# A fourth weight block in the opening: values of the third unit of heads as a plain 32-bit product, with x transposed early and modulated in SBUF

## What is computed

```python
cond = silu(c)
for layer in range(2):
    mod = cond @ ada_w[layer] + ada_b[layer]              # 2048 x 12288 each
    sh1, sc1, g1, sh2, sc2, g2 = split(mod, 6)
    h = rms_norm(x) * (1.0 + sc1) + sh1
    y = even_mixer(h, ...) if layer == 0 else odd_mixer(h, ...)
    x = x + g1 * y
    h = rms_norm(x) * (1.0 + sc2) + sh2
    x = x + g2 * swiglu(h, ffn_w_in[layer], ffn_w_out[layer])
...
def even_mixer(h, w_in, w_out, ...):
    proj = h @ w_in                                        # 2048 x 6144
    aq, ak, av, bq, bk, bv = split(proj, ...)              # 12 blocks of 512 columns
    ...                                                    # heads, in four units of q, k, v
    return concatenate([ya, yb]) @ w_out
```

## Time and profile before

| | |
|---|---|
| median of 3 runs | 2210.9 us (2210.18 to 2211.12) |
| profiled execution: time, span | 2210.82 us, 2209.0 us |
| TensorE busy | 2136.7 us, 97% |
| VectorE busy | 1620.0 us, 73% |
| ScalarE busy | 986.1 us, 45% |
| memory read | 589.62 MB, mean 268 GB/s |

### The profile page before, as it was taken

How to read it: one execution, slowest core, us unless ns; L and a number is a source line. 1 busy time by engine, 2 the same in 40 slices (tenths; PEclk the granted TensorE clock), 3 DMA queues, 4 the chain that set the end, 5 groups by cost and what they waited for, 6 DMA issues and landing times.

```text
span 2209.0 us, 25961 instructions
## 1 busy us (share of the span) xinstructions
PE 2136.7 (97%) x9844; PEld 1755.8 (79%) x9844; DVE 1620.0 (73%) x1681; ACT 986.1 (45%) x1312; POOL 9.4 (0%) x21
## 2 busy tenths in 40 slices
PE   4799999999999999999999999999999999999998
PEld 3578888878888888888887877778888888888886
DVE  6999898988789988777667676686665555455546
ACT  4354444454443344434445456554444344434444
POOL 0000000000000000000000000000000000000000
PEclk7899999999999999999999999999999999999999
DMA  9978879859889999977755533458765555555543
GB/s 395 420 315 313 308 308 375 345 233 363 336 325 369 383 381 379 382 285 289 285 209 233 204 139 125 146 210 323 283 246 191 191 191 190 190 190 190 191 152 152
DMA packets 82557, 593.02 MB, mean 268 GB/s; under 512 B 9424, under 2 KB 9584, under 8 KB 10912
## 3 DMA queue, kind: packets, MB, share of 16 engines
q1 hardware_dynamic: 81216, 587.31, 69.4%
q0 software_dynamic: 1248, 4.44, 0.6%
HBM read 589.62 MB, written 2.10 MB: 268 GB/s over the span
## 4 chain that ended last, share of the span: by engine, by line
PE 83%; DVE 10%; DMA 3%; ACT 3%; DVEq 1%; issue 1%; SPq 0%; ACTq 0%
PE ps L1423 26%; PE ps L1425 26%; PE ps L1424 26%; DVE w_lo L837 3%; DMA ada_raw<-in_ada 2%; PE ps L1411 2%; DVE ada_raw L841 2%; DMA raw<-in_ab_in 1%; PE ps L1451 1%; PE ps L1453 1%; PE ps L1452 1%; ACT w_hi L490 1%; DVE work L981 1%; DVEq L980 0%; ACT ada_raw L594 0%
## 5 line engine op out<-in xcount | busy, mean ns | idle before, releaser
L837 DVE TENSOR_TENSOR w_lo<-raw,w_hi 128x1024 fp32r<-128x1024 f32 x728 | 878.9, 1223 | 409.5 <-ACT w_hi L490 405.2
L490 ACT ACTIVATE w_hi<-raw 128x1024 fp32r<-128x1024 f32 x728 | 762.3, 1059 | 933.8 <-PE ps L1425 753.7
L1423 PE MATMUL ps<-w_hi,xT_hi 128*128 128x512 f32 x1940 | 768.7, 396 | 27.6 <-DVE xT_lo L1141 25.8
L1425 PE MATMUL ps<-w_hi,xT_lo 128*128 128x512 f32 x1940 | 760.0, 392 | 0.0
L1424 PE MATMUL ps<-w_lo,xT_hi 128*128 128x512 f32 x1940 | 759.3, 391 | 0.0
L1423 PEld LDWEIGHTS ps<-w_hi,xT_hi 128*128 128x128 f32 x1940 | 366.7, 189 | 108.3 <-DVE xT_lo L1141 28.0
L1425 PEld LDWEIGHTS ps<-w_hi,xT_lo 128*128 128x128 f32 x1940 | 366.8, 189 | 78.0
L1424 PEld LDWEIGHTS ps<-w_lo,xT_hi 128*128 128x128 f32 x1940 | 367.4, 189 | 74.1
L841 DVE SCALAR_TENSOR_TENSOR ada_raw<-ada_raw,cond 128x2048 f32<-128x2048 f32 x176 | 402.0, 2285 | 8.9 <-DMA ada_raw<-in_ada 7.2
L1423 PE MATMUL ps<-w_hi,hT_hi 128*128 128x512 f32 x896 | 351.5, 392 | 0.1
L1425 PE MATMUL ps<-w_hi,hT_lo 128*128 128x512 f32 x896 | 348.8, 389 | 0.0
(11 more groups left out here) (185 smaller groups left out, 878.2 us busy)
## 6 DMA issues: line engine op xcount, KB each, us to landing
ada_raw<-in_ada SPq DMA_DIRECT2D x176, 1024.0 KB, 6.8
raw<-in_ffn_in SPq DMA_DIRECT2D x176, 1024.0 KB, 5.0
raw<-in_ffn_out SPq DMA_DIRECT2D x88, 1024.0 KB, 5.2
raw<-in_ab_in SPq DMA_DIRECT2D x48, 1024.0 KB, 8.9
raw<-in_swa_in SPq DMA_DIRECT2D x20, 1024.0 KB, 5.1
raw<-in_ab_out SPq DMA_DIRECT2D x16, 1024.0 KB, 7.4
raw<-in_swa_out SPq DMA_DIRECT2D x16, 1024.0 KB, 5.4
spare<-in_ada SPq DMA_DIRECT2D x8, 1024.0 KB, 9.0
```

The lines of the kernel that those rows point to most:

```text
L490: nc.scalar.activation(w_hi[:, p % PAIRS, :, :], raw[:, t % RAW, 2 * (p % 2):2 * (p % 2) + 2, :], ACT.Copy).then_inc(hi_ready, 1)
L837: tt(w_lo[:, p % PAIRS, :, :], raw[:, (p // 2) % RAW, 2 * (p % 2):2 * (p % 2) + 2, :], w_hi[:, p % PAIRS, :, :].bitcast(F32), ALU.subtract ...
L1423: mm(out, hi[:, kt, tok], w_hi[:, q % PAIRS, k, :], start=(kt == 2 * ps0), stop=False)
L1425: last = mm(out, lo[:, kt, tok], w_hi[:, q % PAIRS, k, :], start=False, stop=(kt == 2 * ps1 - 1))
```

## The change

Four things are changed.

*A fourth block.* Unit 2's values are not multiplied in the split form behind unit 1 any more. The opening does this block: four extra quads (`ab_early`) come through slot 3 of `raw` (`EARLY_RAW`), the other weights of unit 0 use a ring of three. TensorE multiplies them straight from `raw` with the modulated x in 32 bits (`early_pair`: four matmuls a round, into banks 6 and 7), without `hi` and `lo`. SP issues the first of these quads in round 0, the others at the end of rounds 2, 4 and 6, each after a wait for `early_used`, which TensorE raises with each group of four products. After the last group ScalarE copies the values to `v_early`, part of `xm`.

*x in SBUF.* `xm` (16 slices of 256 columns; it lies over `hT_lo`, which is used later) takes the transposed x. TensorE transposes the slices of rounds 2 to 7 right behind the three pairs of round 0, through banks 6 and 7, and ScalarE copies each to `xm` (`copy_x0`), between the normalisations. From round 1 on, ScalarE modulates in `xm`, and `xT_hi` and `xT_lo` are made out of it.

*Units 2 and 3 apart.* `AB23` becomes `AB2` (two blocks, 16 pairs) and `AB3` (three blocks). The modulation tiles of the three units are now 12, 8 and 14. The end of unit 1's attention (y to `hT`) and unit 2's key rotation move into unit 3; unit 2's attention lies five pairs later.

*Waits.* Unit 1's fourth quad waits for all eight products (slot 3), unit 0's key transposes wait for `early_copied`.

```diff
@@ sync
             def weights(ph, i, t):
                 sp.wait_ge(lo_ready, LO_CREDIT + 2 * (ph.quad(i, t) - ph.raw_distance(t) + 1))
-                sp.dma_start(raw[:, t % RAW, :, :].rearrange("p a n -> p (a n)"),
-                             T[ph.src][ph.src0 + i * ph.quads + t]).then_inc(raw_landed[t % RAW], 16)
+                if ph is AB1 and t == EARLY_RAW:
+                    sp.wait_ge(early_used, 8)
+                sp.dma_start(raw[:, t % ph.ring, :, :].rearrange("p a n -> p (a n)"),
+                             T[ph.src][ph.src0 + i * ph.quads + t]).then_inc(raw_landed[t % ph.ring], 16)
+
+            def early_weights(s):
+                if s:
+                    sp.wait_ge(early_used, 2 * s)
+                sp.dma_start(raw[:, EARLY_RAW, :, :].rearrange("p a n -> p (a n)"),
+                             T["ab_early"][s]).then_inc(raw_landed[EARLY_RAW], 16)
...
                 for t in range((3 * j + 1) // 2, (3 * j + 4) // 2):
                     weights(AB0, 0, t)
+                if j % 2 == 0:
+                    early_weights(j // 2)
@@ scalar
+            def copy_x0(j):
+
+                act.wait_ge(x0T_done, j + 1)
+                nc.scalar.activation(xm[:, 2 * j:2 * j + 2, :], bank(6 + j % 2).rearrange("p (k s) -> p k s", k=2),
+                                     ACT.Copy).then_inc(x0_copied, 1)
+
             for j in range(8):
                 if j == 7:
                     hi(AB0, 0, 21)
                 act.wait_ge(mods_ready, j + 1)
-                act.wait_ge(x0T_done, j + 1)
-                for k in range(2):
-                    kt = 2 * j + k
-                    o = ps[:, (6 + j % 2) * 512 + k * SEQ:(6 + j % 2) * 512 + (k + 1) * SEQ]
-                    last = nc.scalar.activation(o, o, ACT.Identity, bias=mod[:, 0, 0, kt:kt + 1],
+                if j:
+                    act.wait_ge(x0_copied, j)
+                else:
+                    act.wait_ge(x0T_done, 1)
+                for kt in range(2 * j, 2 * j + 2):
+                    src = xm[:, kt, :] if j else ps[:, 6 * 512 + kt * SEQ:6 * 512 + (kt + 1) * SEQ]
+                    last = nc.scalar.activation(xm[:, kt, :], src, ACT.Identity, bias=mod[:, 0, 0, kt:kt + 1],
                                                 scale=mod[:, 0, 1, kt:kt + 1])
...
                 if j == 0:
-                    normalise(2)
-                    normalise(3)
+                    copy_x0(1)
+                    for c in range(1, 4):
+                        normalise(c)
+                        copy_x0(2 * c)
+                        copy_x0(2 * c + 1)
             hi(AB1, 0, 0)
             copy_v(0)
+            act.wait_ge(early_used, 8)
+            nc.scalar.activation(v_early, bank(6, 2).rearrange("p (t n) -> p t n", t=TT), ACT.Copy).then_inc(early_copied, 1)
@@ tensor
+            def early_pair(j):
+
+                pe.wait_ge(raw_landed[EARLY_RAW], 16 * (j // 2 + 1))
+                for k in range(2):
+                    kt = 2 * j + k
+                    for t in range(TT):
+                        last = mm(bank(6 + t), xm[:, kt, t * P:(t + 1) * P], raw[:, EARLY_RAW, 2 * (j % 2) + k, :],
+                                  start=kt == 0, stop=kt == KT - 1)
+                last.then_inc(early_used, 1)
...
                 pe.wait_ge(x0l_done, j + 1)
                 for b in range(3):
                     pair(AB0, 0, b, j, AB0_SLOT[b], xT_hi, xT_lo, q=3 * j + b)
-                if j < 6:
-                    first_blocks(j + 2)
+                if j == 0:
+                    for c in range(2, 8):
+                        first_blocks(c)
+                    pe.wait_ge(x0_copied, 7)
+                early_pair(j)
@@ phases
-    AB1 = phase(1, 3, 8, 5, src="ab_in", src0=12, evacs=2, lag=4)
-    AB23 = phase(2, 3, 8, 6, src="ab_in", src0=24, evacs=2)
+    AB1 = phase(1, 3, 8, 6, src="ab_in", src0=12, evacs=2, lag=4)
+    AB2 = phase(1, 2, 8, 4, src="ab_in", src0=24, evacs=2)
+    AB3 = phase(1, 3, 8, 7, src="ab_in", src0=32, evacs=2)
```

More of the change, by code:

```diff
@@ L64, with __init__ @@
 class Phase:
-    def __init__(self, prev, n, blocks, pairs, ada, src=None, src0=0, evacs=None, lag=0, tiles_at=None):
+    def __init__(self, prev, n, blocks, pairs, ada, src=None, src0=0, evacs=None, lag=0, tiles_at=None,
+                 ring=RAW, fills=None):
         self.n, self.blocks, self.pairs, self.ada, self.lag, self.tiles_at = n, blocks, pairs, ada, lag, tiles_at
@@ L75, in __init__ @@
         self.ada0 = prev.ada0 + prev.n * prev.ada if prev else 0
-        self.fills = [len(range(s, self.quads, RAW)) for s in range(RAW)]
+        self.ring, self.after = ring, prev.ring if prev else RAW
+        self.fills = fills or [len(range(s, self.quads, RAW)) for s in range(RAW)]
         self.fills0 = [a + prev.n * b for a, b in zip(prev.fills0, prev.fills)] if prev else [0] * RAW
@@ L91, in raw_fills @@
     def raw_fills(self, i, t):
-        s = t % RAW
-        return self.fills0[s] + i * self.fills[s] + t // RAW + 1
+        s = t % self.ring
+        return self.fills0[s] + i * self.fills[s] + t // self.ring + 1
     def raw_distance(self, t):
+        if self.ring < RAW or t < self.after < RAW:
+            return min(self.ring, self.after)
         if t >= RAW or self.quads % RAW == 0:
@@ L154 @@
 C_UNITS = 8
-AB_LATER = (0, 5, 1, 0)
-AB_Q_AT = (2, 17, 13, 12)
-AB_K_AT = (4, 22, 20, 20)
-AB0_SLOT = (1, 2, 0)
+AB_LATER = (0, 5, 1, 5)
+AB_Q_AT = (2, 17, 13, 17)
+AB_K_AT = (4, 22, 4, 22)
+AB_BLOCKS = (3, 3, 2, 3)
+AB0_SLOT = (0, 2, 1)
+EARLY_RAW = 3
 C_LAST = 8 * 5 + 12
@@ L229, in kernel_program @@
         hT_hi = sb("hT_hi", [P, KT, SEQ], F32R)
+        with nc.sbuf_tensor("xm", [P, KT, SEQ], F32) as xm:
+            pass
         hT_lo = sb("hT_lo", [P, KT, SEQ], F32R)
@@ L679, in ab @@
             def ab(i, prev):
-                for n in range(24):
+                for n in range(8 * AB_BLOCKS[i]):
                     if i > 1 or n:
                         hi(*UNIT[i], n)
+                    if i == 3 and n == 0:
+                        ab_stage("hi", 1, "A")
                     ab_stage(AB_ACT.get(n - AB_LATER[i]), i - 1, prev)
@@ L989, in ab_rope @@
                     dve.wait_ge(pair_used, USED_CREDIT + AB0.pair(0, 23 + b))
-                dst, slot = nat_k if b else nat, (i + b) % 2 if i else AB0_SLOT[b + 1]
+                dst, slot = nat_k if b else nat, ab_slot(i, b) if i else AB0_SLOT[b + 1]
                 for t in range(TT):
@@ L1140, in residue @@
                 dve.wait_ge(x0h_done, j + 1)
-                tt(xT_lo[:, 2 * j:2 * j + 2, :], bank(6 + j % 2).rearrange("p (k s) -> p k s", k=2),
+                tt(xT_lo[:, 2 * j:2 * j + 2, :], xm[:, 2 * j:2 * j + 2, :],
                    xT_hi[:, 2 * j:2 * j + 2, :].bitcast(F32), ALU.subtract).then_inc(x0l_done, 1)
@@ L1184, in ab @@
             def ab(i, prev):
-                for n in range(24):
+                late = AB_LATER[i]
+                for n in range(8 * AB_BLOCKS[i]):
                     lo(*UNIT[i], n)
@@ L1188, in ab @@
                         ab_rope(0, n // 2)
+                    if i == 3 and n == 0:
+                        ab_stage("lo", 1, "A")
+                    if i == 3 and n == 3:
+                        ab_rope(2, 1)
                     ab_stage(AB_DVE.get(n - AB_LATER[i]), i - 1, prev)
@@ L1619, in ab @@
             def ab(i, prev):
-                for b in range(3):
-                    if b == (i > 1):
+                for b in range(AB_BLOCKS[i]):
+                    if i < 3 and b == i - 1:
                         pe.wait_ge(v_copied, i)
+                    elif i == 3:
+                        pe.wait_ge(evacuated, EVAC_CREDIT + 5 + b)
                     else:
@@ L1626, in ab @@
                         n = 8 * b + p
-                        pair(*UNIT[i], b, p, (i + b) % 2, xT_hi, xT_lo)
+                        pair(*UNIT[i], b, p, ab_slot(i, b), xT_hi, xT_lo)
                         ab_stage(AB_PE.get(n - AB_LATER[i]), i - 1, prev)
@@ L1856, in layouts @@
         "ada_bias": ada_b.reshape(2, 6, KT, P).transpose(3, 0, 1, 2),
-        "ab_in": np.concatenate([first, ab[order[3:]].reshape(-1, P, 4 * NT)]),
+        "ab_in": np.concatenate([first, ab[order[3:8] + order[9:]].reshape(-1, P, 4 * NT)]),
+        "ab_early": ab[order[8]],
         "ab_out": ab_out,
```

70 lines of the change are left out of this document (42 added, 28 removed).

## The result

The changed kernel takes **2255.57 us** (median of four runs, 2254.56 to 2256.1) against 2210.54 (four runs, 2209.68 to 2211.12): a ratio of 1.0203 with a 95% interval of 1.0186 to 1.0221. It is 45 us, or 2%, slower. Its profiled execution spans 2253.8 us against 2209.0, 44.8 more. The forecast was 2244.5 with a range of 2224 to 2268.

What follows compares the result with a forecast made beforehand. TensorE was taken as bound by DMA landings in the opening, then busy itself: 2209.0 - 21.8 + 3.5 + 45 + 7 = 2242.7 us of span, plus 1.8, forecast 2244.5 us; range 2224 to 2268.

Steps and rivals of the forecast that it cites:

- Term 3: Opening: new loads hold SP until TensorE's 32-bit products finish; 11.3 us more each after rounds 4 and 6.
- Term 4: Opening, ScalarE: copies waiting for early transposes delay round 1's modulation by 10 us; round 3 begins at 79 instead of 56.16.
- T7: Moment VectorE begins round 7's first tile: forecast 155.6 against 110.76 before, plus 44.8 us, taken as 45.
- Term 1: Units 1 to 3: eight split pairs of 2.72 us removed, minus 21.8 us of TensorE; VectorE loses 9.8 us of residues.
- the stretch behind the opening: Sign of a right forecast: after the opening, TensorE has few waits and a stretch shorter by 15 to 20 us.
- Term 2: 32-bit products: 3.5 us a round; seven of eight groups lie in TensorE waits, only the last adds 3.5 us.
- Term 5: Units 1 to 3 with less VectorE slack: 5 us of TensorE lost in unit 1, 2 in unit 3; bounds 2 to 14.
- over 14 us of waits: Sign of a wrong forecast: TensorE waiting over 14 us for residues in units 1 to 3, their loss taken too small.
- A: Rival: SP's wait ends before DMA runs dry, opening pays only 10.0 us; 2204.5 to 2209.5 us; 6% including passing loads.
- D: Rival: compiler or queue lets tiles pass the waiting load; same time as the free held queue, counted in its 6%.
- B: Rival: ScalarE reaches round 1's modulation without the 10 us delay; 2228.5 us; 12% with other ways to halve the opening's cost.
- C: Rival: TensorE runs all its work in held-queue rounds at the lower clock, three times 9 us more; 2271 us; 12%.

Runs made afterwards that it cites:

- The experiment on the order: The changed kernel with SP issuing 32-bit loads 1, 2 and 3 at the end of rounds 3, 5 and 7 instead of 2, 4 and 6: 2226.94 us.
- both edits: The changed kernel with loads 1 to 3 issued later and the early transposes spread ahead of and between round 0's pairs: 2219.16 us, ratio 1.0036.
- the tiles at 10, 10 and 14: The changed kernel with late loads, spread transposes, unit 1's splits ahead, and two modulation tiles moved from unit 1 to unit 2: 2210.3 us.

## Why the prediction was right, and where it was off

**Term 3, SP held by TensorE: right, mechanism and size.** Forecast were T(j+1) = Tj + 25.1 for j = 4 and 6, measured 24.91 and 24.62. SP was released 109.02 - 91.49 = 17.5 us after T4 and 17.3 after T6 (forecast 17.6), the tile landed 7.4 us after that (7.5), 7.0 after its own issue. The 5.0 us that the forecast took from the earlier trace rows for an empty queue are the median of 176 loads, and that row does not say that their queue was empty; the three held loads of this run, each into an idle queue, landed in 4.8, 4.9 and 4.8 us, so the size held. The experiment on the order puts the price of a hold at 9.3 us, where the term had 11.3 over a round of before. The difference is no error in the sum: without the hold the extra load costs the round its own bytes, and with both edits the rounds came 14.9 us apart.

**Term 4, the early transposes: right, T3 = 79 for 77.98.** ScalarE reached the modulation at 52.32 (forecast 53.1), the first 32-bit products ran at the lower clock as assumed (6.51 us), and T4 and T6 came at 91.49 and 130.21 (92.2 and 130.5). T7 was forecast at 155.6 and measured at 154.83. Alone, the transposes cost 9 us.

**Term 1: right in size, but not what it was worth.** The block did go, but the units became only 4.8 us shorter. The forecast had VectorE's sums and took them for a matter of 7 us. Of the signs that it named, this one failed: the stretch behind the opening was to be 15 to 20 us shorter.

**Term 2: one group too few.** The duration was right, 3.45 us a group. The sentence that failed is the one that seven of the eight groups lie in waits of TensorE. Round 7's first pair starts at 173.0, directly behind round 6's products, while VectorE's residue was done at 170.5 (T7 + 15.7; before it was 126.40 - 110.76 = 15.6): 2.5 us of round 6's group are on the path as well. The groups of rounds 2 and 4 do just fit, with 0.3 us of waiting left behind them, because that step takes 17.7 us in a round with tiles behind it (73.88 - 56.16). Round 7 has none, its residue comes 2.1 us sooner, and round 6's pairs had begun at the lower clock.

**Term 5: too small, the step that failed.** Forecast 7 us (bounds 2 to 14), measured 225.5 - (230.3 - 21.8) = 17.0 us. It has two parts. Waits: 12.3 - 1.7 = 10.6 us. The clock: of such a wait the forecast counted only the wait. Here is the longest, TensorE and then VectorE ahead of it:

```profile
233.60 0.90 PE L1458 MATMUL ps<-ident,gate 128*128 128x128 f32 x3 [4.59 <-DVE gate L1125]
...
235.58 0.63 PE L1470 MATMUL ps<-w_hi,xT_hi 128*128 128x512 f32 x1
```

```profile
219.29 1.23 DVE L879 TENSOR_TENSOR w_lo<-raw,w_hi 128x1024 fp32r<-128x1024 f32 x1 [4.34 <-ACT w_hi L518]
...
224.06 0.42 DVE L1019 TENSOR_TENSOR gate<-ps,rope_ab 128x256 f32<-128x256 f32 x1
...
229.65 2.28 DVE L883 SCALAR_TENSOR_TENSOR ada_raw<-ada_raw,cond 128x2048 f32<-128x2048 f32 x1
...
232.99 0.55 DVE L1125 COPY gate<-ps 128x384 f32<-128x384 f32 x1
```

VectorE does a rotation from 224.06, a residue, a tile at 229.65, a residue, and then the copy at 232.99 that TensorE has waited for since 229.0; behind it eleven matmuls stand 0.43 us apart instead of 0.23, 2.3 us more. Behind the waits of 2.56 and 3.21 us come another 1.6 each. Together that is 16.1 of the 17.0 us; 0.9 I can't place. Of the loss, the copy of the early values in ScalarE's way accounts for 5 to 7 us by the spans (5.0 alone, 7.0 with both edits in place). The rest moved about with the tiles, and no placing that was tried made it small.

The first of these rows shows something that the sums leave out: VectorE itself stood idle for 4.34 us, 10 us ahead of that copy, for a weight split that ScalarE had behind eight exponentials of the attention (3.3 us). In the kernel before this wait was 2.15 us, because a tile of 2.29 us lay in the gap. With the tiles at 10, 10 and 14 a tile lies there again: VectorE waits 2.15 us, and TensorE 1.18 instead of 3.75. So a part of this loss is the order of work between ScalarE and VectorE and not VectorE's sum.

My comparison of sums (75.0 of VectorE against 76.4 of TensorE) took as a small risk what left almost no slack: with 9.8 us of residues and 21.8 us of products gone, the forecast's own terms give VectorE 207.6 - 9.8 = 197.8 of 208.5 us, 95%, where it had been 207.6 of 230.3, 90%. VectorE's work comes in lumps of 4.4 + 2.3 us, TensorE's needs for it every 2.7. The run with the two tiles moved has 248.0 of 276 us between 134 and 410, as before (248.9). These runs suggest that 90% is about the limit for this order of work. It is not shown: none took work from VectorE, and none filled its idle gaps while it left the rest in place.

The sum, then: the span missed by 11.1 us. T7 gives -0.9, the second group +2.5, the units +10.0 and all that lies behind them -0.3; unrounded they add up to 11.2. The time fell inside the range through the bounds of the other terms; the largest miss was beyond its own bound of 14. The sign set for that, over 14 us of waits, did not show it, since TensorE waited only 12.3 us: the clock took the rest.

**The rivals.** A (the held queue is free) is out: three holds, 27.8 us. D (the order is not held) is out with it. B (the transposes fit) is out: 10.1 us of idling on VectorE at 55.04. C, the slow clock, was half seen. Three rounds do begin at the lower clock after 11.5 us of idling, but it comes back within the first two pairs (in round 3 at 85.4, 3.4 us after the start), and the products of those rounds run at the upper level, 2.4 GHz (3.59 us). By the Trainium skill (TensorE: Matmul & The Clock Gate, HAM oscillation) work that follows such a wait starts cold each time. The trace agrees for the start of all three rounds (3.4, 5.9 and 5.1 us at the lower clock), and shows the clock back inside each one. The example of the Trainium skill has bursts of about 2 us; here TensorE's work in a round is 13 us long, so that pattern does not give C's time, though the prediction said it would. Cold starts did cost time, but in units 1 to 3 and not in the opening. In the opening VectorE paces the rounds; in the units waits of 2.6 to 4.6 us were followed by 8 to 14 slow matmuls on the path.

## What to carry to other kernels

A load that waits for a consumer holds every load behind it on its queue. Before a prefetch is added, find the latest place in the queue where it still arrives in time, and put it behind all that the next stage needs: here three instructions moved gave 28 of 45 us. Work handed to an idle engine is free only if what it waits for is early too: here copies that waited for transposes held up the one step that everybody needed, and that cost 9 us. And work taken off the bounding engine is a gain only as far as the second engine has slack at the grain of its largest pieces: with VectorE 90% busy, 22 us of removed products shortened the units by 5 us. That the grain and not the order is the reason was not shown.
